# Weight blocks of 1 MB that lie contiguously, seven slots that hold a piece first raw and then as its low part, six rounded slots

## What is computed

```python
# layer 0: adaLN; heads of latent attention beside a gated short convolution; then SwiGLU
z = h @ w_in                          # q latent, ckv, kpe, gb, gc, u
q = rms(rms(q_lat) @ w_qb); k, v = split(ckv @ w_kvb)
o = concat(attend(q, k, v), gb * conv3(gc * u)) @ w_o
x = x + gate * o
x = x + gate * (silu(h @ w_g) * (h @ w_u)) @ w_down          # width 2816
# layer 1: adaLN; Conformer convolution (31 taps) between two projections; then experts
x = x + gate * (silu(layernorm(conv31(glu(h @ w_pw1 + b)))) @ w_pw2 + b)
for e in range(8):                                             # width 3584, top 2 of 8
    out += gates[:, e] * (silu(h @ w_g[e]) * (h @ w_u[e])) @ w_down[e]
x = x + gate * out
```

## Time and profile before

| | |
|---|---|
| median of 3 runs | 1750.07 us (1747.69 to 1752.91) |
| profiled execution, span from first to last instruction | 1752.1 us |
| mean granted TensorE clock | 0.945 |
| busy: PE, DVE, ACT | 89%, 70%, 56% of the span |
| read from HBM | 469.75 MB, 269 GB/s over the span |
| piece loads (SP's queue) | 464.43 MB in 336176 packets |

### The profile page before, as it was taken

One profiled execution on the slowest core, in us unless ns is written; L12 is line 12 of the kernel. 1 busy time (PEld: TensorE's weight loads), 2 busy tenths in 40 slices (PEclk: granted clock), 3 DMA queues, 4 the chain that ended last, 5 costly groups with the idle time before them and its releaser, 6 DMA issues.

```text
span 1752.1 us, 20909 instructions
## 1 busy us (share of the span) xinstructions
PE 1564.9 (89%) x7157; PEld 1235.7 (71%) x7157; DVE 1231.9 (70%) x1171; ACT 973.2 (56%) x978; POOL 18.6 (1%) x25
## 2 busy tenths in 40 slices
PE   3758878999598877999999999999999999999996
PEld 1536556888476555788788788788788788788784
DVE  1444555544558726788888888888888888888886
ACT  1232424443435533677677677676676776776673
POOL 0000000000000000000000000000000000000000
PEclk9778889999798977999999999999999999999998
DMA  7554685565344515899999999999999999999992
GB/s 273 184 189 173 221 277 175 190 192 192 120 145 144 199 41 192 284 362 334 315 366 335 316 366 336 318 366 333 318 366 336 308 366 334 324 366 318 327 364 100
DMA packets 340212, 471.62 MB, mean 269 GB/s; under 512 B 13023, under 2 KB 274861, under 8 KB 340158
## 3 DMA queue, kind: packets, MB, share of 16 engines
q1 hardware_dynamic: 336176, 464.43, 77.8%
q0 software_dynamic: 1216, 4.28, 0.7%
q10 hardware_dynamic: 2766, 2.22, 0.4%
HBM read 469.75 MB, written 1.13 MB: 269 GB/s over the span
## 4 chain that ended last, share of the span: by engine, by line
PE 82%; DVE 10%; ACT 4%; DMA 2%; issue 1%; ACTq 0%; POOL 0%; DVEq 0%; POOLq 0%
PE bank L1395 23%; PE bank L1397 23%; PE bank L1396 23%; DVE low L1307 2%; PE bank L1407 2%; PE bank L1770 2%; ACT high L741 2%; PE bank L1884 2%; PE bank L1912 1%; DVE low L814 1%; DVE hid L1159 1%; PE bank L1424 1%; DMA x<-x_sample 1%; PE bank L1443 1%; ACT high L468 1%
## 5 line engine op out<-in xcount | busy, mean ns | idle before, releaser
L1307 DVE TENSOR_TENSOR low<-raw,high 128x2048 fp32r<-128x2048 f32 x333 | 760.6, 2292 | 150.5 <-ACT high L741 137.6
L741 ACT ACTIVATE high<-raw 128x2048 fp32r<-128x2048 f32 x333 | 634.6, 1915 | 111.9 <-PE bank L1397 111.3
L1395 PE MATMUL bank<-high,slotH 128*128 128x512 f32 x896 | 359.1, 401 | 26.2 <-DVE low L1307 25.4
L1397 PE MATMUL bank<-high,slotL 128*128 128x512 f32 x896 | 356.9, 398 | 0.0
L1396 PE MATMUL bank<-low,slotH 128*128 128x512 f32 x896 | 356.0, 397 | 0.0
L1395 PE MATMUL bank<-high,upH 128*128 128x512 f32 (+1 forms) x550 | 227.6, 414 | 4.4 <-DVE upL L944 2.8
L1395 PEld LDWEIGHTS bank<-high,slotH 128*128 128x128 f32 x896 | 169.1, 189 | 73.7 <-DVE low L1307 33.8
L1397 PE MATMUL bank<-high,upL 128*128 128x512 f32 (+1 forms) x550 | 217.3, 395 | 0.0
L1396 PE MATMUL bank<-low,upH 128*128 128x512 f32 (+1 forms) x550 | 215.3, 391 | 0.0
L814 DVE TENSOR_TENSOR low<-raw,high 128x2048 fp32r<-128x2048 f32 (+3 forms) x59 | 132.3, 2250 | 106.8 <-ACT high L468 106.6
L1397 PEld LDWEIGHTS bank<-high,slotL 128*128 128x128 f32 x896 | 169.3, 189 | 40.8
(11 more groups left out here) (228 smaller groups left out, 1221.2 us busy)
## 6 DMA issues: line engine op xcount, KB each, us to landing
raw<-moe_gu SPq DMA_DIRECT2D x448, 512.0 KB, 5.4
raw<-moe_down SPq DMA_DIRECT2D x112, 1024.0 KB, 6.6
raw<-ada_w SPq DMA_DIRECT2D x48, 1024.0 KB, 7.0
raw<-ffn_gu SPq DMA_DIRECT2D x44, 512.0 KB, 4.9
raw<-ffn_down SPq DMA_DIRECT2D x11, 1024.0 KB, 4.9
raw<-conv_pw SPq DMA_DIRECT2D x16, 512.0 KB, 4.4
raw<-w_in SPq DMA_DIRECT2D x6, 1024.0 KB, 8.0
raw<-w_o SPq DMA_DIRECT2D x4, 1024.0 KB, 6.8
```

The source lines that it names most:

```text
L741: a.activation(high[:, m % SPLITS, :], raw[:, n % RAWS, :], ACT.Copy).then_inc(S("high_ready"), 1)
L1307: v.tensor_tensor(low[:, m % SPLITS, :], raw[:, n % RAWS, :], high[:, m % SPLITS, :].bitcast(F32), ALU.subtract).then_inc(S("low_ready"), 1)
L1395: pe.matmul(out, xh, wh, start=start, stop=False)
L1397: return pe.matmul(out, xl, wh, start=False, stop=stop)
```

## The change

The host packs the dense pieces into one array `dense` [107, 128, 2048] and those of the experts into `moe` [8, 42, 128, 2048], so that a piece is a contiguous block of 1 MB in the layout of its slot; each is loaded by one transfer with one row of 8 KB per partition. The raw ring has seven slots; `low` is a tensor over the same addresses, and DVE writes the low part over the raw piece that it reads. The high ring has six slots. A split piece's slot is released when PE has used the piece. `vTpad` shares its space with upH and upL, `probT` is part of `hid`, `rope_t` part of `gate`.

```diff
-RAWS = 6
-SPLITS = 3
+RAWS = 7
+SPLITS = 6
...
-        raw = sb("raw", [P, RAWS, PIECE])
+        ring = ExitStack()
+        raw = sb("raw", [P, RAWS, PIECE], where=ring)
+        ring.close()
+        low = sb("low", [P, RAWS, PIECE], F32R)
         high = sb("high", [P, SPLITS, PIECE], F32R)
-        low = sb("low", [P, SPLITS, PIECE], F32R)
...
-        upH = sb("upH", [P, 2, UC, TILES * P], F32R)
-        upL = sb("upL", [P, 2, UC, TILES * P], F32R)
+        ph = ExitStack()
+        upH = sb("upH", [P, 2, UC, TILES * P], F32R, where=ph)
+        upL = sb("upL", [P, 2, UC, TILES * P], F32R, where=ph)
+        ph.close()
+        ph = ExitStack()
+        vTpad = sb("vTpad", [P, SCC, TILES, P + 2], where=ph)
+        ph.close()
+        sb("up_space", [P, 4 * UC * TILES * P])
...
-        rope_t = probT[:, 0, 0:2, :].rearrange("p a b -> p (a b)").rearrange("p (h d) -> p h d", h=HEADS)
+        probT = hid[:, 0:4, :].rearrange("p k n -> p (k n)").rearrange("p (g m n) -> p g m n", g=2, m=4)
+        rope_t = gate[:, 1, 0:HEADS * ROPE].rearrange("p (h d) -> p h d", h=HEADS)
...
+        def low_slot(m):
+
+            if m < N_SPLIT:
+                return STREAM[SPLIT[m]] % RAWS
+            return (m - N_SPLIT + N_DENSE) % RAWS
...
                     if last in DNUM:
                         sp.wait_ge(S("direct_used"), DNUM[last] + 1)
                     else:
-                        sp.wait_ge(S("low_ready"), NUM[last] + 1)
+                        sp.wait_ge(S("piece_used"), NUM[last] + 1)
+                w = width(piece)
+                sp.dma_start(raw[:, slot, 0:w], t["dense"][n, :, 0:w]).then_inc(arrived, 16)
...
-                    sp.dma_start(dst[:, :, 0, :], v[:, :, :, c0:c0 + UNIT]).then_inc(arrived, 16)
-                    sp.dma_start(dst[:, :, 1, :], v[:, :, :, D_FFE + c0:D_FFE + c0 + UNIT]).then_inc(arrived, 16)
+                sp.dma_start(raw[:, slot, :], t["moe"][bass.ds(e, 1), i]).then_inc(arrived, 16)
...
                         expert_load(e, first, i,
-                                    lambda: sp.wait_ge(S("low_ready"), e * PER_E + (split + i - RAWS + 1)))
+                                    lambda: sp.wait_ge(S("piece_used"), e * PER_E + (split + i - RAWS + 1)))
...
-                v.tensor_tensor(low[:, n % SPLITS, 0:w], raw[:, STREAM[SPLIT[n]] % RAWS, 0:w],
+                v.tensor_tensor(low[:, STREAM[SPLIT[n]] % RAWS, 0:w], raw[:, STREAM[SPLIT[n]] % RAWS, 0:w],
                                 high[:, n % SPLITS, 0:w].bitcast(F32), ALU.subtract).then_inc(S("low_ready"), 1)
...
-                                           w_slot(low, m % SPLITS, (KH, 512))[:, k, :], kk == 0, kk == KT - 1)
+                                           w_slot(low, low_slot(m), (KH, 512))[:, k, :], kk == 0, kk == KT - 1)
```

More of the change, by code:

```diff
@@ L170, in build @@
         work = sb("work", [P, 3 * HEADS * P], where=ph)
-        probT = sb("probT", [P, 2, 4, P], where=ph)
-        vTpad = sb("vTpad", [P, SCC, TILES, P + 2], where=ph)
         ph.close()
@@ L356, in experts @@
                 for i in range(lead, PER_E if lead else 0):
-                    expert_load(0, first, i, lambda: sp.wait_ge(S("low_ready"), split + i - RAWS + 1))
+                    expert_load(0, first, i, lambda: sp.wait_ge(S("piece_used"), split + i - RAWS + 1))
                 with sp.Fori(1 if lead else 0, EXPERTS) as e:
@@ L371, in _ @@
             sp.wait_ge(S("y_out"), 32)
-        def loads_of(piece):
-            return 2 if piece[0] in ("ffn", "pw1") and piece[1] != "d" else 1
         def arrived_value(n):
-            return 16 * sum(loads_of(ORDER[m]) for m in range(n % RAWS, n + 1, RAWS))
-        def slot_total(slot):
-            return 16 * sum(loads_of(ORDER[m]) for m in range(slot, N_DENSE, RAWS))
+            return 16 * (n // RAWS + 1)
         def expert_value(first, i):
[L385 to L389, removed]
+            return 16 * ((first + i) // RAWS + 1), 16 * (PER_E // RAWS)
         @block.gpsimd
@@ L1213, in first_expert @@
                 v.wait_ge(S("high_ready"), m + 1)
-                v.tensor_tensor(low[:, m % SPLITS, :], raw[:, n % RAWS, :],
+                v.tensor_tensor(low[:, n % RAWS, :], raw[:, n % RAWS, :],
                                 high[:, m % SPLITS, :].bitcast(F32), ALU.subtract).then_inc(S("low_ready"), 1)
@@ L1511, in _ @@
                                    w_slot(high, n % SPLITS, (2, HEADS * QK))[:, c, cols],
[L1512 removed]
+                                   w_slot(low, low_slot(n), (2, HEADS * QK))[:, c, cols], c == 0, c == 1)
                 if tt == 0:
@@ L1530, in keys_values @@
                                high[:, n % SPLITS, hh * 512:(hh + 1) * 512],
-                               low[:, n % SPLITS, hh * 512:(hh + 1) * 512], True, True)
+                               low[:, low_slot(n), hh * 512:(hh + 1) * 512], True, True)
                 if j < 2:
@@ L2004, in constants, with rows_of, gate_up_rows, down_rows @@
     return c
+def rows_of(w, kh, c0, cw):
+    return w[kh * KH * P:(kh + 1) * KH * P, c0:c0 + cw].reshape(KH, P, cw).transpose(1, 0, 2)
+def gate_up_rows(w, ff, u, kh):
+    import numpy as np
+    return np.stack([rows_of(w, kh, u * UNIT, UNIT), rows_of(w, kh, ff + u * UNIT, UNIT)], axis=2)
+def down_rows(w, u):
+    return w[u * UNIT:(u + 1) * UNIT].reshape(UC, P, D).transpose(1, 0, 2)
+def dense_piece(inputs, piece):
+    kind = piece[0]
+    if kind == "ada":
+        (l, c), kh = piece[1], piece[2]
+        return rows_of(inputs["ada_w"][l], kh, c * 512, 512)
+    if kind == "win":
+        c0, cw = W_CHUNK[piece[1]]
+        return rows_of(inputs["w_in"][0], piece[2], c0, cw)
+    if kind == "qb":
+        return inputs["w_qb"][0].reshape(2, P, HEADS * QK).transpose(1, 0, 2)
+    if kind == "kvb":
+        return inputs["w_kvb"][0]
+    if kind == "ffn":
+        if piece[1] == "d":
+            return down_rows(inputs["ffn_down"][0], piece[2])
+        return gate_up_rows(inputs["ffn_gu"][0], D_FF, piece[2], "ab".index(piece[1]))
+    if kind == "pw1":
+        return gate_up_rows(inputs["conv_pw1"][0], D, piece[2], "ab".index(piece[1]))
+    w = inputs["w_o"][0] if kind == "wo" else inputs["conv_pw2"][0]
+    return rows_of(w, piece[2], piece[1] * 512, 512)
 def kernel(**inputs):
@@ L2014 @@
     arrays["table"] = constants()
+    dense = np.zeros((N_DENSE, P, PIECE), np.float32)
+    for n, piece in enumerate(ORDER):
+        rows = np.asarray(dense_piece(inputs, piece)).reshape(P, -1)
+        dense[n, :, 0:rows.shape[1]] = rows
+    moe = np.empty((EXPERTS, PER_E, P, PIECE), np.float32)
+    for e in range(EXPERTS):
+        w_gu, w_down = np.asarray(inputs["moe_gu"][0, e]), np.asarray(inputs["moe_down"][0, e])
+        for i, (kind, u) in enumerate(STREAM_E):
+            rows = down_rows(w_down, u) if kind == "d" else gate_up_rows(w_gu, D_FFE, u, "ab".index(kind))
+            moe[e, i] = rows.reshape(P, PIECE)
+    arrays["dense"], arrays["moe"] = dense, moe
     t = {name: nc.dram_tensor(name, arr.shape, F32, kind="ExternalInput").ap() for name, arr in arrays.items()}
```

33 lines of the change are left out of this document (9 added, 24 removed).

## The result

The changed kernel took 1757.25 us (median of 20 runs, 1752.35 to 1762.49) against 1748.18 (20 runs of the kernel before, 1744.63 to 1753.59). The ratio is 1.0044, 95% interval 1.0034 to 1.0055: slower, as forecast (1757.6).

The account below looks back on a forecast made before the run. It took PE in the experts to wait on the program order of ACT and DVE, not on ring or transfers. Terms -1.0 + 4.5 + 4.0 = +7.5 us gave 1759.6 as span, 1757.6 as median; range 1753.5 to 1762, chance 0.55.

Parts of the forecast that it names:

- 0 for six rounded slots: Experts and dense part: six rounded slots for three gain 0, PE's waits come from program order; bounds -24.8 and 0.
- 0 for the shared slot: Low part over the raw slot: later slot release costs 0, a load having 16.0 us of PE work to cover it.
- The rival by which the ring was the wait: Experts: the deep ring takes PE's waits away, 24.8 us in all, 1733 us (half of it 1745); chance 0.10.
- the one by which the transfers were the limit: Experts: larger packets give back PE's idle time, some 21 us, 1737 us; chance 0.04.
- Late slots: Rival: splitting and landing overrun 16.0 us at each expert's edge, one or two us per expert, 1766 to 1773; chance 0.09.
- First expert piece: covered with 1.2 us to spare: First expert piece: load lands some 5 us later, yet splitting ends at 656.4, ahead of DVE's residual at 657.62; cost 0.
- win/1/0: -1.0: Dense part's only load on the chain: its slot comes free one ada half earlier, gain 1.0 us; bounds 0 and -2.
- The start: +4.5 by x at 27.2: Start: x lands after all seven 8 KB-row loads, at 27.2 instead of 22.7 us; cost 4.5, bounds 5.5 and 0.
- The gate bias: +4.0: At 212.39 us: POOL's two transfers wait in turn behind 8 KB packets of 0.34 us; cost 4.0, bounds 5 and 0.

Follow-up runs that it names:

- rings only: Kernel before with only the new rings (seven raw/low slots, six rounded, release on use), old layout and transfers: 1746.54 us, ratio 0.9993.
- order: Kernel before, shallow ring kept, with part (b, 2) moved ahead of silu(1) and (b, 4) ahead of the backR copy: 1714.15 us, ratio 0.9809.
- start held: Changed kernel, where SP waits for x's landing before its third load: 1746.81 us, ratio 0.9981 to the kernel before.

## Why the prediction was right

*The experts: 0 for six rounded slots, 0 for the shared slot.* Shown. The period and PE's waits are the old ones; "rings only" holds 1, and "order" removes PE's waits with the shallow ring in place. The rival by which the ring was the wait is out, and so is the one by which the transfers were the limit: five times fewer packets changed nothing in the period, and an expert of 126.30 us is reached with the old transfers. Late slots were not seen either: loads land in 4.8 us (median; 5.1 at most from 1125 to 1206 us), against 16.0 of room.

*First expert piece: covered with 1.2 us to spare.* ACT's copy ran at 654.95 and DVE's subtraction ended at 659.2, ahead of the residual at 660.98. The cover holds with 1.8 us.

```profile
656.89 2.29 DVE L1170 TENSOR_TENSOR low<-raw,high 128x2048 fp32r<-128x2048 f32 x1 [16.96 <-ACT high L660]
660.98 2.36 DVE L843 TENSOR_TENSOR hid<-bank,gate 128x1024 f32<-128x1024 f32 x2 [1.79 <-PE bank L1353]
```

*win/1/0: -1.0.* The mechanism was right, the load left the chain, but the term was mis-sized. The profile of after goes from 0.1 us behind (the copy at 115.95 against 115.85) to 0.3 ahead (129.45 against 129.76), a gain of 0.4 us only. The load lands at 128.20, but ACT's copy starts at 129.45, behind the evacuation that stands before it in ACT's order; what was waiting for the load now waits for the convolution's own steps:

```profile
128.87 0.58 ACT vals L506
129.45 1.80 ACT high L424
```

*The start: +4.5 by x at 27.2.* Measured +4.84, x at 27.56. The two parts of the argument hold, packets in turn and x behind all seven loads. I had passed over the second consequence, that rows of 4 KB do the same. That it counts in full is shown by "start held". The size was in part luck: 9.48 MB at the 380 GB/s that I took, from the same 1.7 us on as at 358, land at 26.6 us, not at the 27.2 I wrote, which makes the cost 3.9. In the trace it was 7.34 + 2.19 = 9.53 MB, at 369 GB/s reckoned in that way.

*The gate bias: +4.0.* The landing grew by 2.9 us; the low part behind it came at 226.52 instead of 223.82, 2.7 later, though the profile of after had been ahead by 0.2 us at 206 and was behind by 3.7 at PE's next step in the chain (237.20 against 233.51): 3.9 in the stage. That 3.9 is so near to the 4.0 is luck: 2.9 of it is the landing, and the other 1.0 comes in the stretch in which the clock was 0.81 instead of 0.91, a cost that the prediction didn't have. The Trainium skill (DMA: Bandwidth & Descriptors, Queues, rings and completion order) has an engine drain a packet of some 9 to 17 descriptors from one ring before it turns to the next. By it I had estimated 3.2 us, which is nearer to the 2.9 than my 4.1. But its descriptors are the rows that the profile counts as packets, and neither the counts (169 to 168, 147 to 148, 552 to 553) nor the order of the single packets (270 of 272 changes of queue) show such a grouping. The nearer size is thus no support for the rule. What made my term too large is the price of queue 1's packet. Its mean, with the small semaphore packets counted as in the 0.085 of before, was 66.1% x 16 engines x 4 us / 147 = 0.29 us between 217 and 221, not 0.34: 16 x (0.29 - 0.085) = 3.3.

*The sum.* +7.5 was forecast. The steps measured in the profiles give 4.8 + 3.9 - 0.4 = 8.3, the means differ by 8.6 and at equal clock by 10.0; that last difference of 1.7 is within the error and was not traced. The median of 1757.25 lies 0.35 us from the forecast, which is partly luck: I took the span as the time (1.8 us lie outside it) and put the median 2.0 below it.

## What to carry to other kernels

Here a queue that was always full set the price of every small transfer beside it, by the size of its packets; before rows are made longer, look for the small transfers on the chain and for how many packets stand ahead of them, and hold the big queue back for those few microseconds. A DMA share of 1.00 and 105 us of waits on a ring say nothing while the engine that bounds the kernel doesn't wait for them: two places in a program's order were worth three to four times what the whole change cost. Compare single profiles only together with their granted clocks.

## What the runs showed of the hardware

- Two full queues were served packet by packet in turn at every size that ran here: 552 to 553 at 2 KB, 358 to 361 at 4 KB, 169 to 168 at 8 KB, 147 to 148 with POOL's queue.
- ACT's own DMA issues at the start took longer, the longer the rows of the loads beside them: with rows of 8 KB one took 4.14 us and the four behind it 2.1 to 2.4 each; with 4 KB it was 0.8 and then 1.3 to 1.5, in the kernel before 0.6 to 0.8, and with the start held 0.4 to 0.8. The cause is not shown. ACT's program stands still in that time; here it had nothing else to do, and waited another 4.58 us for x behind it.
- 0.001 of mean granted clock went with 1.15 us of this kernel's time. In most of the dense part the clock goes up and down between its two levels, 1.2 and 2.4 GHz (0.5 and 1.0 of the full clock), in phases that fall differently from run to run: from 30 to 70 us the mean was 0.70 in the profile of before and 0.83 in that of after, which hid all but 0.4 us of the start's loss in that pair (the same small step of POOL starts at 75.96 us in the chain, against 75.55).

```profile
30.00:70.00 40.00, 28.85 (x147) 19.17 (x146) 14.32 (x22) 9.65 (x13) 0.00 (x0) 0.70 0.75 272
```

```profile
30.00:70.00 40.00, 26.34 (x154) 18.34 (x155) 16.45 (x28) 10.92 (x15) 0.71 (x1) 0.83 0.54 210
```
